# Mixture-of-experts block: both experts' sums in memory become one, and each scatter waits for the one in front of it

## The chip, the cores and the metric

The kernel runs on 1 core of one Trainium2 chip. The metric is the device time of one execution in microseconds (us), the median of several runs. A core has TensorE (PE in the rows, PEld its weight loads), VectorE (DVE), ScalarE (ACT), GpSimd (POOL) and SyncE (SP), and 16 DMA engines that serve the queues of SP, ACT and POOL. A "q" behind an engine's name (SPq, POOLq) is its sequencer.

## What is computed

Two transformer blocks over 512 tokens of width 1024. The first has a convolution and sparse attention and then a mixture of experts; the second has two mixers and two dense feed-forward nets. The change is in the experts:

```python
scores = jax.nn.sigmoid((t @ w_router).astype(jnp.float32))
_, eidx = lax.top_k(scores + router_bias.astype(jnp.float32), TOP_K_EXPERTS)
...
def expert_block(args):
    e, toks, gs = args
    xb = t[toks]
    return swiglu(xb, w1[e], w3[e], w2[e]) * gs[:, None]
...
routed = jax.ops.segment_sum(out.reshape(rows, D), row_tok, num_segments=n_tok)
shared = swiglu(t, ws1, ws3, ws2)
return (routed + shared).reshape(B, S, D)
```

Each token's row is the sum of what its 8 experts give for it, so the results of different experts are added into the same rows. 512 tokens times 8 experts over 64 experts are 64 rows for an expert on average, and up to 128 are taken at once.

## The kernel before

**One expert.** The 64 experts run one after the other in a loop that is written out (`step(n, i)`, i = 0 throughout; functions of one expert have n as argument). For expert n: GpSimd gathers its tokens' rows from memory (`gather`, L2113, tile XG, four buffers), TensorE turns them (`pe_xt`, L2007), ScalarE and VectorE split them into a high and a low part (XTh, XTl), TensorE multiplies by the up and gate weights (`pe_up`), VectorE makes silu times gate times up (`dve_hid`, L2072, tile HG, which needs the token's gate from `gate_column`, L2100, tile GS, made by GpSimd), TensorE turns that (`pe_ht`, L2032) and multiplies by the down weights (`pe_down`), ScalarE copies the 128 x 1024 result out of PSUM (`act_y`, L2091, tile YS, two buffers) and GpSimd adds it into memory (`scatter`, L2127, an indirect DMA with an addition; rows whose index is out of bounds are left out). All multiplications are three passes of 128 x 512 matmuls (L298 to L300) over weights in two parts (wh, wl), split by ScalarE (L192) and VectorE (L197) out of a ring of 12 chunks (eraw). SyncE loads the ring in pairs of chunks, 1 MB each (L1975), each when the chunks that stood there have been split: three pairs for an expert.

**Why two sums.** Even experts are added into `ysum[0]`, odd ones into `ysum[1]` (both `expert_sum` in the rows). Scatter n waits until that of n - 2, into the same sum, has landed (`y_out[s]`), then for its rows (`y_ready`). So two scatters can be in flight, into different memory. `act_y` of expert n waits for the landing of scatter n - 2 too, since it writes the same buffer of YS.

**The order on GpSimd** is fixed: in step n first `gate_column(n + 1)`, then `gather(n + 4)`, then `scatter(n)`. What stands behind scatter n on that engine, the gate of expert n + 2 and the gather of expert n + 5, is only issued after it.

**The last experts and what is over.** From n = 60 on, `more_gather` takes the place of `gather`: it copies an index column, drains (L2147) and gathers (L2153) rows for tokens beyond an expert's 128 + 64 places. These "more" blocks run after the 64 experts; with this data there are three (L2433 scatters them, each waited for, `more_gate` L2423 makes their gates). Then GpSimd waits for all scatters and tells `rows_whole`.

**Behind the experts.** Before the experts SyncE writes zeros into both sums (L1580, 8 DMAs of 512 KB). After `rows_whole` it reads both sums back (L2396, 8 DMAs of 512 KB in 4 quarters of the columns, tile YF), VectorE adds the two (L2541, 4 times 128 x 1024), TensorE turns each quarter (L2561, 8 transposes each), VectorE adds it into the residual X (`back`, L2527, twice for each quarter), ScalarE and VectorE split X (L2584, `x2_low` L2532, twice for each quarter), and the first multiplication of the second block starts. TensorE runs dummy matmuls (`keep_clock(3)`, L471) between `rows_whole` and the first transposes.

## Time and profile before

| | us |
|---|---|
| median of 3 runs | 2372.37 (2371.32 to 2376.65) |
| the profiled execution | 2377.54 |
| its span, first to last instruction | 2375.7 |
| TensorE busy in the span | 2256.5 (95%) |
| VectorE busy | 1536.6 (65%) |
| ScalarE busy | 1198.8 (50%) |
| GpSimd busy | 286.1 (12%) |
| mean granted TensorE clock | 0.983 of full |

The profiled execution took 2377.54 us, 5.17 us more than the median of the runs; its span leaves 1.84 us around it. The experts' loop takes from about 465 us (first scatter) to 1064 us (64th), the three blocks behind it until 1105 us, the second transformer block the rest. In the experts' loop the DMA engines' mean busy share is 9 tenths or more in every slice of the page; elsewhere it is mostly 1 to 3 tenths. In the rows further down, times are from the start of the span. A row of the timeline gives start, duration, engine, line, operation and tiles, and in brackets how long the engine was idle before it and what ended that. "DMA to landing" is the time from the start of the issuing instruction until all of its data has landed. The engine time of an indirect DMA on POOL is the making of its descriptors.

### The profile page before, as it was taken

How to read it: one execution, taken by the hardware profiler on the slowest of the kernel's cores; microseconds unless marked ns; L12 is line 12 of the kernel's file. 1: busy time of each engine (PE TensorE's matmuls, PEld its weight loads, DVE VectorE, ACT ScalarE, POOL GpSimd, SP SyncE). 2: the span in 40 equal slices, each digit the busy share in tenths (PEclk: the TensorE clock that was granted, in tenths of full speed). 3: DMA queues.
4: the chain of work that ended last, by engine and by line, in shares of the span. 5: the costliest groups of instructions: out<-in, count | busy, mean ns of one | idle time of the engine just before them, and what ended most of it. 6: DMA issues, size and time to landing. Idle time of an engine off the chain costs nothing.

```text
span 2375.7 us, 30540 instructions
## 1 busy us (share of the span) xinstructions
PE 2256.5 (95%) x10226; PEld 1760.5 (74%) x10226; DVE 1536.6 (65%) x2363; ACT 1198.8 (50%) x1774; POOL 286.1 (12%) x248
## 2 busy tenths in 40 slices
PE   7999999899999999985999999999999789999997
PEld 5776666778888888874766788888788557888885
DVE  7788766899999999985564643333452766433344
ACT  4432444588888888874334332333222763323333
POOL 0000000344334433431000000000020000000000
PEclk9998999999999999998999999999999999999999
DMA  8511245799999999995210132223222001322332
GB/s 330 176 59 58 80 169 172 266 354 397 388 393 387 391 392 393 391 334 156 80 63 18 62 107 96 97 97 107 89 98 98 19 27 61 116 98 92 102 106 80
DMA packets 107615, 415.70 MB, mean 175 GB/s; under 512 B 20305, under 2 KB 32849, under 8 KB 82784
## 3 DMA queue, kind: packets, MB, share of 16 engines
q1 hardware_dynamic: 87408, 378.47, 42.5%
q0 software_dynamic: 19648, 34.73, 5.9%
q8 instruction: 71, 1.16, 0.2%
q10 hardware_dynamic: 432, 0.87, 0.1%
q14 instruction: 56, 0.46, 0.1%
HBM read 409.23 MB, written 43.65 MB: 191 GB/s over the span
## 4 chain that ended last, share of the span: by engine, by line
PE 77%; DVE 9%; issue 5%; ACT 4%; DMA 2%; DVEq 2%; POOLq 0%; SPq 0%; POOL 0%; ACTq 0%
PE PS L298 22%; PE PS L300 21%; PE PS L299 21%; PE PS L714 3%; DVE wl L197 2%; PE PS L2007 2%; ACT wh L192 2%; PE PS L736 2%; PE PS L725 1%; DMA ada_wa<-wada 1%; DMA expert_sum<-YS,YIXC 1%; PE PS L2032 1%; DVE XTl L2060 1%; PE PS L1245 1%; DVEq L1285 1%
## 5 line engine op out<-in xcount | busy, mean ns | idle before, releaser
L197 DVE TENSOR_TENSOR wl<-raw,wh 128x1024 fp32r<-128x1024 f32 x239 | 292.5, 1225 | 357.2 <-ACT wh L192 351.0
L298 PE MATMUL PS<-HTh,wh 128*128 128x512 f32 x1248 | 499.9, 401 | 6.0 <-ACT V L881 2.2
L299 PE MATMUL PS<-HTl,wh 128*128 128x512 f32 x1248 | 487.8, 391 | 0.0
L300 PE MATMUL PS<-HTh,wl 128*128 128x512 f32 x1248 | 487.6, 391 | 0.0
L197 DVE TENSOR_TENSOR wl<-eraw,wh 128x1024 fp32r<-128x1024 f32 x384 | 457.7, 1219 | 16.6 <-ACT wh L192 13.6
L192 ACT ACTIVATE wh<-raw 128x1024 fp32r<-128x1024 f32 x239 | 252.0, 1056 | 369.9 <-PE PS L300 346.1
L192 ACT ACTIVATE wh<-eraw 128x1024 fp32r<-128x1024 f32 x384 | 392.6, 1054 | 17.0 <-PE PS L300 14.7
L298 PEld LDWEIGHTS PS<-HTh,wh 128*128 128x128 f32 x1248 | 235.3, 189 | 72.2 <-issue 13.6
L299 PEld LDWEIGHTS PS<-HTl,wh 128*128 128x128 f32 x1248 | 235.5, 189 | 50.2 <-issue 3.4
L300 PEld LDWEIGHTS PS<-HTh,wl 128*128 128x128 f32 x1248 | 235.3, 189 | 49.8
L298 PE MATMUL PS<-wh,XTh 128*128 128x512 f32 x536 | 221.1, 412 | 4.0 <-DVE wl L2192 2.8
L300 PE MATMUL PS<-wh,XTl 128*128 128x512 f32 x536 | 210.4, 392 | 0.0
L299 PE MATMUL PS<-wl,XTh 128*128 128x512 f32 x536 | 209.3, 390 | 0.0
L2127 POOL DMA_INDIRECT expert_sum<-YS,IDX x64 | 115.0, 1796 | 343.2 <-ACT YS L2091 211.3
L298 PE MATMUL PS<-AFh,wh 128*128 128x512 f32 x352 | 138.5, 394 | 0.0
L300 PE MATMUL PS<-AFh,wl 128*128 128x512 f32 x352 | 137.0, 389 | 0.0
L299 PE MATMUL PS<-AFl,wh 128*128 128x512 f32 x352 | 137.0, 389 | 0.0
L947 ACT ACTIVATE AFh<-AFf 128x512 f32 (+1 forms) x44 | 27.8, 632 | 182.4 <-DVEq L957 182.4
L298 PEld LDWEIGHTS PS<-wh,XTh 128*128 128x128 f32 x536 | 100.8, 188 | 23.4 <-DVE wl L2192 4.0
L300 PEld LDWEIGHTS PS<-wh,XTl 128*128 128x128 f32 x536 | 100.6, 188 | 22.2
L299 PEld LDWEIGHTS PS<-wl,XTh 128*128 128x128 f32 x536 | 101.2, 189 | 16.9
L298 PE MATMUL PS<-wh,HHh 128*128 128x512 f32 x268 | 105.6, 394 | 4.5 <-DVE HHl L2509 2.8
(412 smaller groups left out, 3439.7 us busy)
## 6 DMA issues: line engine op xcount, KB each, us to landing
eraw<-wstream SPq DMA_DIRECT2D x192, 1024.0 KB, 9.9
raw<-wstream SPq DMA_DIRECT2D x240, 512.0 KB, 3.3
ada_w<-wada SPq DMA_DIRECT2D x20, 512.0 KB, 5.9
eraw<-wexp SPq DMA_DIRECT2D x9, 1024.0 KB, 6.6
ada_wb<-wada SPq DMA_DIRECT2D x2, 2048.0 KB, 15.5
ada_l<-wada SPq DMA_DIRECT2D x8, 512.0 KB, 3.4
ada_g<-wada SPq DMA_DIRECT2D x2, 2048.0 KB, 10.3
expert_sum<-LM SPq DMA_DIRECT2D x8, 512.0 KB, 6.4
```

The costliest lines, as they stand in the source:

```text
L192: nc.scalar.activation(wh[:, ci % RING, :], src, ACT.Copy).then_inc(split_high, 1)
L197: nc.vector.tensor_tensor(wl[:, ci % RING, :], src, wh[:, ci % RING, :].bitcast(F32), ALU.subtract).then_inc(split_done, 1)
L298: nc.tensor.matmul(o, lh, rh, start=start, stop=False)
L299: nc.tensor.matmul(o, lh, rl, start=False, stop=False)
L300: return nc.tensor.matmul(o, ll, rh, start=False, stop=stop)
L714: mm = nc.tensor.matmul(PS[:, sbank(u, m), 0:P * (j + 1)], q[:, j * P:(j + 1) * P], k[:, 0:P * (j + 1)], start=x == 0, stop=x == len(prods ...
L725: mm = nc.tensor.transpose(PS[:, 4 + u % 2, kb * P:(kb + 1) * P], E_[:, u % 3, 0, kb * P:(kb + 1) * P], const("ident"))
L736: mm = nc.tensor.matmul(o, values(h, kb), Pt[:, u % 2, kb * P:(kb + 1) * P], start=kb == 0, stop=kb == j)
L947: nc.scalar.activation(ah(n, i), a_[:, n % 2, :], ACT.Copy).then_inc(s_h, 1)
L1245: nc.tensor.matmul(PS[:, 5 + n % 3, 0:P * (j + 1)], QI[b:b + HD, t, j * P:(j + 1) * P], KI[b:b + HD, 0:P * (j + 1)], start=True, stop=True ...
L2007: mm = nc.tensor.transpose(PS[:, 2 + m // 4, (m % 4) * P:(m % 4) * P + P], XG[:, n % 4, m * P:(m + 1) * P], const("ident"))
L2127: pool.indirect_dma_start(out=ysum[s], out_offset=bass.IndirectOffsetOnAxis(ap=IDX[:, 4 * n:4 * n + 1], axis=0), in_=YS[:, s, :], in_offse ...
```

## The change

One sum `ysum` takes the place of two. Scatter n now waits first for its rows (`y_ready`) and then until scatter n - 1 has landed (`y_out[1 - s]`), which is the other buffer's counter. Four DMAs write zeros, four read the sum back, the four additions on VectorE are gone, and TensorE's transposes wait for a quarter's landing. YF is half as large and stands 4096 places higher. The waits of `act_y` on its own buffer are as before.

```diff
--- before.py
+++ after.py
@@ -1563,7 +1563,7 @@
             LS = nc.alloc_sbuf_tensor_at("LS", [P, E], F32, offset=RSTD_AT + 4 * 448)
             h2rows = nc.dram_tensor("h2rows", (S, XW), F32).ap()
             blocks = nc.dram_tensor("more_blocks", (P, 3), I32).ap()
-            ysum = [nc.dram_tensor(f"expert_sum{s}", (S, D), F32).ap() for s in range(2)]
+            ysum = nc.dram_tensor("expert_sum", (S, D), F32).ap()
             EMPTY = 4103.0
 
             @stage("sp")
@@ -1576,9 +1576,8 @@
                     sp.dma_start(*expert_pair(j, EXPERT0 + j)).then_inc(expert_arrived[j // 2], 16)
                 sp.wait_ge(sem("lm_zero"), 1)
                 for tb in range(NB):
-                    for s in range(2):
-                        sp.dma_start(ysum[s].rearrange("(b p) (c e) -> b p c e", p=P, e=P)[tb],
-                                     LM[:].unsqueeze(1).broadcast_to([P, DT, P])).then_inc(sem("sum_zero"), 16)
+                    sp.dma_start(ysum.rearrange("(b p) (c e) -> b p c e", p=P, e=P)[tb],
+                                 LM[:].unsqueeze(1).broadcast_to([P, DT, P])).then_inc(sem("sum_zero"), 16)
                 sp.wait_ge(sem("gates_whole"), 1)
                 for h in range(2):
                     sp.dma_start(h2rows.rearrange("(h t p) d -> p h t d", h=2, p=P)[:, h, :, D:XW],
@@ -1706,7 +1705,7 @@
 
             def list_main(dve):
 
-                dve.wait_ge(sem("sum_zero"), 32 * NB)
+                dve.wait_ge(sem("sum_zero"), 16 * NB)
                 for b in range(2):
                     nc.vector.tensor_copy(spread_of(LM, lower)[:, b, :, :, :], ranked_of(LL, lower)[:, b, :, :, :])
                 back = LL[upper, ::-1].rearrange("p (a l H e) -> p H a l e", a=2, l=4, H=2)
@@ -1959,7 +1958,7 @@
             HHh = place("HHh", [P, 2, 256], 9472, F32R)
             HHl = place("HHl", [P, 2, 256], 9984, F32R)
             YS = nc.alloc_sbuf_tensor_at("YS", [P, 2, D], F32, offset=HT_AT)
-            YF = place("YF", [P, 2, 4, NB, 256], 3072)
+            YF = place("YF", [P, 4, NB, 256], 7168)
 
             @stage("sp")
             def _(sp):
@@ -2116,15 +2115,15 @@
 
             def scatter(pool, n, i):
                 s = n % 2
-                if n >= 2:
-                    pool.wait_ge(y_out[s], 16 * (n // 2))
-                    pool.sem_inc(passed_pool, 1)
-                elif n == 0:
-                    pool.wait_ge(sem("sum_zero"), 32 * NB)
-                    pool.sem_inc(passed_pool, 1)
                 pool.wait_ge(y_ready, i * 4 + n + 1)
                 pool.sem_inc(passed_pool, 1)
-                pool.indirect_dma_start(out=ysum[s], out_offset=bass.IndirectOffsetOnAxis(ap=IDX[:, 4 * n:4 * n + 1], axis=0),
+                if n:
+                    pool.wait_ge(y_out[1 - s], 16 * ((n + 1) // 2))
+                    pool.sem_inc(passed_pool, 1)
+                else:
+                    pool.wait_ge(sem("sum_zero"), 16 * NB)
+                    pool.sem_inc(passed_pool, 1)
+                pool.indirect_dma_start(out=ysum, out_offset=bass.IndirectOffsetOnAxis(ap=IDX[:, 4 * n:4 * n + 1], axis=0),
                                         in_=YS[:, s, :], in_offset=None, bounds_check=S - 1, oob_is_err=False,
                                         compute_op=ALU.add).then_inc(y_out[s], 16)
 
@@ -2392,9 +2391,8 @@
                 sp.wait_ge(sem("rows_whole"), 1)
                 sp.wait_ge(sem("ya_free"), 1)
                 for q in range(4):
-                    for s in range(2):
-                        sp.dma_start(YF[:, s, q, :, :], ysum[s].rearrange("(b p) (q d) -> q p b d", p=P, q=4)[q]
-                                     ).then_inc(ya_in[q], 16)
+                    sp.dma_start(YF[:, q, :, :], ysum.rearrange("(b p) (q d) -> q p b d", p=P, q=4)[q]
+                                 ).then_inc(ya_in[q], 16)
 
                 with sp.Fori(EXPERT0 // RING + 1, CHUNKS // RING - 6 * E // RING) as i:
                     for c in range(RING):
@@ -2430,7 +2428,7 @@
                     more_gather(pool, p + 2, code_of(p + 2, i), i)
                     pool.wait_ge(ov["y"], i * GROUP + (p + 2))
                     pool.sem_inc(passed_pool, 1)
-                    pool.indirect_dma_start(out=ysum[0], out_offset=bass.IndirectOffsetOnAxis(ap=YIXC[:, y:y + 1], axis=0),
+                    pool.indirect_dma_start(out=ysum, out_offset=bass.IndirectOffsetOnAxis(ap=YIXC[:, y:y + 1], axis=0),
                                             in_=YS[:, p % 2, :], in_offset=None, bounds_check=S - 1, oob_is_err=False,
                                             compute_op=ALU.add).then_inc(ov["out"], 16)
                     pool.wait_ge(ov["rows"], i * (16 * GROUP) + 16 * (p + 3))
@@ -2537,8 +2535,6 @@
                     nc.vector.tensor_scalar(lamc[:, 5:6], col("g_sub"), 1.0 - LAMBDA_INIT, None, ALU.mult)
                     dve.drain().then_inc(sem("lam_p"), 1)
                 for q in range(4):
-                    dve.wait_ge(ya_in[q], 32)
-                    nc.vector.tensor_tensor(YF[:, 0, q, :, :], YF[:, 0, q, :, :], YF[:, 1, q, :, :], ALU.add).then_inc(sem("ya_whole"), 1)
                     if second and q:
                         x2_low(2 * q - 2)
                         x2_low(2 * q - 1)
@@ -2554,12 +2550,12 @@
                 keep_clock(3)
                 for m in range(DT):
                     if m % 2 == 0:
-                        pe.wait_ge(sem("ya_whole"), m // 2 + 1)
+                        pe.wait_ge(ya_in[m // 2], 16)
                     if m >= 4:
                         pe.wait_ge(sem("ya_read"), m - 3)
                     for tb in range(NB):
                         mm = nc.tensor.transpose(PS[:, SUM_BANK[m % 4], tb * P:(tb + 1) * P],
-                                                 YF[:, 0, m // 2, tb, m % 2 * P:(m % 2 + 1) * P], const("ident"))
+                                                 YF[:, m // 2, tb, m % 2 * P:(m % 2 + 1) * P], const("ident"))
                     mm.then_inc(sem("ya_t"), 1)
 
         if second:
```

GpSimd, the scatters of experts 0 to 3 and what lies between them (XG is the gathered rows, GS the gate column, y_out0 and y_out1 count the landings of even and odd experts' scatters). Before:

```order
L2127 DMA expert_sum0<-YS_117,IDX_92 512x1024 [waits sum_zero,y_ready]
L2100 COPY GS_95<-XG_110 128x1 [waits xg_in2]
L2113 DMA XG_110<-h2rows,IDX_92 128x1088 [waits xg_in1,xt_ps,gate_at]
L2127 DMA expert_sum1<-YS_117,IDX_92 512x1024 [waits y_ready]
L2100 COPY GS_95<-XG_110 128x1 [waits xg_in3]
L2113 DMA XG_110<-h2rows,IDX_92 128x1088 [waits xg_in2,xt_ps,gate_at]
L2127 DMA expert_sum0<-YS_117,IDX_92 512x1024 [waits y_out0,y_ready]
```

Now:

```order
L2126 DMA expert_sum<-YS_117,IDX_92 512x1024 [waits y_ready,sum_zero]
L2099 COPY GS_95<-XG_110 128x1 [waits xg_in2]
L2112 DMA XG_110<-h2rows,IDX_92 128x1088 [waits xg_in1,xt_ps,gate_at]
L2126 DMA expert_sum<-YS_117,IDX_92 512x1024 [waits y_ready,y_out0]
L2099 COPY GS_95<-XG_110 128x1 [waits xg_in3]
L2112 DMA XG_110<-h2rows,IDX_92 128x1088 [waits xg_in2,xt_ps,gate_at]
L2126 DMA expert_sum<-YS_117,IDX_92 512x1024 [waits y_ready,y_out1]
```

No instruction has moved; the odd expert's scatter, which waited for no landing or for that of two experts ago, now waits for the even one's just in front of it, and the other way round.

VectorE, behind the experts (YF is the sum read back, X the residual, HTl its low part). Before:

```order
L2537 TENSOR_SCALAR lamc<-C 128x1
L2541 TENSOR_TENSOR YF<-YF 128x1024 [waits ya_in0]
L2527 SCALAR_TENSOR_TENSOR X<-PS,cond,X 128x512 [waits ya_t] x2
L2541 TENSOR_TENSOR YF<-YF 128x1024 [waits ya_in1]
L2532 TENSOR_TENSOR HTl<-X,HTh 128x512 [waits x2h] x2
L2527 SCALAR_TENSOR_TENSOR X<-PS,cond,X 128x512 [waits ya_t] x2
```

Now:

```order
L2535 TENSOR_SCALAR lamc<-C 128x1
L2525 SCALAR_TENSOR_TENSOR X<-PS,cond,X 128x512 [waits ya_t] x2
L2530 TENSOR_TENSOR HTl<-X,HTh 128x512 [waits x2h] x2
L2525 SCALAR_TENSOR_TENSOR X<-PS,cond,X 128x512 [waits ya_t] x2
```

The additions have gone from between the others, here the first two of four.

## Rows read from the trace of the kernel before

**Rows 1.** Start of scatter 1 to 59: length, PE, PEld, DVE, ACT, POOL, clock, DMA, GB/s.
```profile
475.22:1024.97 549.75, 546.23 (x2674) 448.78 (x2673) 529.21 (x595) 488.38 (x581) 219.61 (x176) 1.00 1.02 387
```

**Rows 2.** Timeline of POOL, a scatter in the loop and the gate behind it.
```profile
760.75 2.08 POOL L2127 DMA_INDIRECT expert_sum<-YS,IDX  x1 [6.29 <-ACT YS L2091]
762.27 1.71 POOL L2100 COPY GS<-XG 128x1 f32<-128x1 f32 x1
```

**Rows 3.** DMA issues from 470 to 530 us: count, size, median us to landing.
```profile
eraw<-wstream SPq DMA_DIRECT2D x18, 1024.0 KB, 7.7
expert_sum<-YS,IDX POOLq DMA_INDIRECT x6, 9.4
```

**Rows 4.** DMA issues from 530 to 710 us.
```profile
eraw<-wstream SPq DMA_DIRECT2D x58, 1024.0 KB, 9.5
expert_sum<-YS,IDX POOLq DMA_INDIRECT x19, 9.2
```

**Rows 5.** DMA issues from 710 to 890 us.
```profile
expert_sum<-YS,IDX POOLq DMA_INDIRECT x19, 9.6
```

**Rows 6.** The scatters of the three blocks behind the experts (L2433), shortest, median, longest.
```profile
DMA to landing us min/median/max: 5.1/6.0/6.3
```

**Rows 7.** Timelines of ACT and POOL: the rows are ready, the scatter starts.
```profile
503.51 1.03 ACT L2091 ACTIVATE YS<-PS 128x1024 f32<-128x1024 f32 x1 [1.11 <-PE PS L300]
505.42 2.18 POOL L2127 DMA_INDIRECT expert_sum<-YS,IDX  x1 [6.62 <-DVE HG L2072]
```

**Rows 8.** Timeline of DVE: the hidden row that needs the gate just made.
```profile
768.62 0.47 DVE L2072 SCALAR_TENSOR_TENSOR HG<-SG,GS,PS 128x256 f32<-128x256 f32 x1
```

**Rows 9.** Timeline, the last experts: scatters 61 and 63, ACT's copy 63, gate, hidden row.
```profile
1052.68 1.60 POOL L2127 DMA_INDIRECT expert_sum<-YS,IDX  x1 [0.31 <-issue]
...
1062.41 1.03 ACT L2091 ACTIVATE YS<-PS 128x1024 f32<-128x1024 f32 x1 [4.61 <-DMA expert_sum<-YS,IDX]
...
1064.27 1.56 POOL L2127 DMA_INDIRECT expert_sum<-YS,IDX  x1 [8.04 <-ACT YS L2091]
1065.24 1.55 POOL L2423 COPY GS<-XG 128x1 f32 x1
...
1069.16 0.48 DVE L2506 SCALAR_TENSOR_TENSOR HG<-SG,GS,PS 128x256 f32<-128x256 f32 x1
```

**Rows 10.** Scatter 63 (L2127) alone, issued at 1064.27: shortest, median, longest.
```profile
DMA to landing us min/median/max: 5.5/5.5/5.5
```

**Rows 11.** Timeline of SP, its first issue after the zeros.
```profile
413.67 0.91 SPq L1584 DMA_DIRECT2D h2rows<-G  x2
```

**Rows 12.** Timeline behind the experts: reading back, adding, turning, first matmul of block 2.
```profile
1108.08 8.78 SPq L2396 DMA_DIRECT2D YF<-expert_sum  x8
1108.11 4.66 PE L471 MATMUL PS<-K 128*128 128x512 f32 x6 [10.05 <-POOLq L2445]
1115.30 1.23 DVE L2541 TENSOR_TENSOR YF<-YF 128x1024 f32<-128x1024 f32 x1 [9.61 <-DMA YF<-expert_sum]
1116.58 1.97 PE L2561 MATMUL PS<-K,YF 128*128 128x128 f32 x8 [3.81 <-DVE YF L2541]
1117.74 1.60 DVE L2527 SCALAR_TENSOR_TENSOR X<-PS,cond,X 128x512 f32<-128x512 f32 x2 [1.21 <-PE PS L2561]
1130.46 0.77 PE L298 MATMUL PS<-HTh,wh 128*128 128x512 f32 x1
1131.09 1.47 DVE L2532 TENSOR_TENSOR HTl<-X,HTh 128x512 fp32r<-128x512 f32 x2
```

**Rows 13.** Landing of the eight reads of YF: shortest, median, longest.
```profile
DMA to landing us min/median/max: 3.4/8.1/10.1
```

**Rows 14.** Timeline of PE in the tail: an idle time and a matmul soon after it.
```profile
1055.05 0.44 PE L2032 MATMUL PS<-K,HG 128*128 128x128 f32 x2 [2.74 <-DVE HG L2072]
1057.65 0.63 PE L299 MATMUL PS<-wl,HHh 128*128 128x512 f32 x1
```

**Rows 15.** Page, costliest groups: the matmuls of L299 in the loop; busy us, mean ns.
```profile
L299 PE MATMUL PS<-wl,XTh 128*128 128x512 f32 x536 | 209.3, 390 | 0.0
```

## The prediction, made before the changed kernel was run

> **What bounds the kernel now.** I read first the busy time of each engine in the stretch that the change touches, the experts' loop. From the start of scatter 1 to that of scatter 59 are 549.75 us; TensorE is busy for 546.23 of them at a granted clock of 1.00 [rows 1]. That is 549.75 / 58 = 9.48 us for an expert, and TensorE sets it. The DMA engines are full at the same time (share 1.02, 387 GB/s) [rows 1], with the stream of weights above all. The reader is to see that both are full, and that GpSimd, with 219.61 us, is not.
>
> Then GpSimd's timeline, for what a step does there: scatter at 760.75, gate of the expert after next from 762.27 to 763.98 [rows 2]. The scatter waits for its rows, not for a landing. Then the DMA issues by stretch, for how long a scatter is under way: median 9.4 us, 9.2, 9.6 [rows 3 to 5]. This is the number that matters: a landing takes almost exactly as long as an expert. With two sums nobody waits for it, since the wait is for the landing of two experts ago, 9.5 us more. With one sum it becomes a link of a chain.
>
> **The wait that is added.** Scatter n may only start when n - 1 has landed, so two scatters stand at least a landing and a wake-up apart. The wake-up is not shown for a landing; its nearest row is the wake-up by ScalarE: the copy YS ends at 503.51 + 1.03 = 504.54, the scatter starts at 505.42 [rows 7], 0.88 us. The instructions between are the same two waits and the setting of a register, so I take 0.88.
>
> The landing under the new pace is shown by no row. Bounds: 6.0 us, the median of the three scatters behind the loop, which have little beside them [rows 6], and 9.6, the worst stretch [rows 5]. I take 9.2 [rows 4]. It is nearest to the stretches in the loop, since the same 3 MB of weights an expert stay beside it. At a step of some 10 us the stream asks for 6% less, which speaks for the low one of the three medians; but between 470 and 530 us the stream's own transfers landed in 7.7 us, against 9.5 later, and the scatters were no faster there, 9.4 against 9.2 [rows 3, 4]. So I don't go below 9.2.
>
> A step then takes 9.2 + 0.88 = 10.08 us in place of 9.48, 58 of them 584.6 us: **+34.9 us** in GpSimd's time at scatter 59.
>
> **What is queued behind the wait.** On GpSimd the gate of expert n + 2 and the gather of n + 5 stand behind scatter n. The gather has three experts of time. The gate has less: it ended at 763.98, and VectorE's hidden row that needs it started at 768.62 [rows 2, 8], 4.6 us of slack. GpSimd falls behind by 0.6 us an expert, so the slack is used up after some 8 experts; from then on TensorE waits for VectorE's hidden row about 0.6 us in each. Does the slack of 4.6 us come off the sum? No: in the tail GpSimd is already what the others wait for (TensorE idle for 2.74 us until HG, whose gate stands behind scatter 61 [rows 14]), so its lag is passed on whole.
>
> **The tail.** Scatters 60 and 61 stand behind drains of `more_gather` and are apart by more than a landing already. Scatter 62 followed 61 closely and must now wait for it. ScalarE's copy 63 waits for the same landing and starts at 1062.41 [rows 9]; scatter 62 then starts at about 1063.2. Alone it lands in 5.5 us [rows 10], at 1068.7, and scatter 63 starts at 1069.6 in place of 1064.27 [rows 9]: 5.3 us later. The gate behind it ended 2.5 us after the scatter's start, which makes 1072.1, and the hidden row that needs it ran at 1069.16 [rows 9]: 2.9 us at least. The first extra block's gather and scatter stand behind too. I take **+5 us**, between 3 and 7. The three extra blocks wait for each landing already; nothing there.
>
> **What is removed.** Zeroing: 4 DMAs less for SyncE. That gives nothing: what SyncE issues next waits for the router's gates and starts at 413.67 [rows 11], whether it has issued 4 or 8 before. If the gates came sooner than the eighth, the four would be worth their issue time, some us.
> Reading back: the first addition starts at 1115.30, 7.2 us after the first of 8 reads was issued [rows 12], as two of them must land and share the engines with the rest. A single one lands in 3.4 us [rows 13], at 1111.5. TensorE's dummies end at 1112.77 [rows 12], so its transposes start there, not at 1116.58: -3.8 us. Further on VectorE sets the pace: from 1117.74 to 1132.56 [rows 12] it runs 8 `back`, 8 low parts and 3 additions of 1.23. Without these it is done 3.7 + 3.8 = 7.5 us earlier. TensorE, whose last transposes no longer queue behind an addition, can start the next matmuls (1130.46 before) up to 11 us earlier, but needs the last low parts soon. I take **-9 us**, between -7 and -11.
>
> **Sum.** +34.9 + 5 - 9 = +31 us. On the profiled execution (2377.5) this gives 2408; that one was 5.2 us over the median of the runs, so on the median 2372.4 + 31 = **2403 us**.
>
> **Rivals.**
> A, the landing gives way. If scatters land faster once each runs alone in its sum, the chain may be shorter than TensorE's step. It decides at 9.48 - 0.88 = 8.6 us a landing: below that nothing is lost in the loop, and the tail and the end leave 5 - 9 = -4 us to -7 us: about 2366, faster. For it: alone, 6.0 us [rows 6], so a third of a landing is made by company, and a slower loop makes the stream thinner: some feedback is certain. Against it: in the loop a scatter never had much company of another scatter, and no stretch has a median below 9.2. The Trainium skill, "DMA: Bandwidth & Descriptors", Anatomy of one DMA (SWDGE path), gives about 2.0 us plus bytes / 436e3 for such a DMA; by that rule, as an estimate, 262 KB for 64 rows would land in 2.6 us, the wait would be free and the sum would be A's 2366. The trace doesn't agree even for scatters nearly alone (5.1 to 6.3 us) [rows 6]. 0.13.
>
> B, the landing doesn't change at all and is 9.6 us [rows 5] throughout: 58 x 10.48 = 607.8, +58, with the rest +54: 2426. This is the upper end of my own forecast.
>
> C, the clock. Today an idle time of 2.74 us was followed by matmuls at 0.63 us each [rows 14], where the mean of such matmuls is 0.39 [rows 15]. If 0.6 us idle an expert were enough for that, some nine matmuls an expert would cost 0.2 us more each, 1.8 us, of which 0.6 lie in the wait: +70 us more, about 2473. Against it: the granted clock is 1.00 with the small gaps of today [rows 1]. 0.04.
>
> D, the lag isn't passed on: the tail's drains of many us could swallow the 4.6 us that GpSimd is behind. Then 2398, inside the range.
>
> **Numbers.** The forecast (landing 8.75 to 9.6 us) has 0.80; A 0.13; C and what else is slower 0.07. The range: at 8.75 us, 58 x 9.63 = 558.5, +8.8 + 5 - 9 = +5, 2377; at 9.6 us 2426. The time of no change is reached at a landing of 8.67 us. A measurement of this kernel can tell about 0.2%, 4.7 us, from no change. Faster by over that (most of A) 0.10; within 0.08 (the rest of A, landings near 8.7); slower 0.82.
>
> **What would show it.** In the profile after: scatters 10.1 us apart; landings of 9 us or more; POOL idle before L2126 until DMA expert_sum, no longer until ACT YS; VectorE's HG waiting for POOL GS some 50 times for about 0.6 us, and TensorE for HG; DMA share in the loop about 0.95; clock 1.00. Behind the experts YF's reads landing within some 8 us of the first issue, and the first matmul of block 2 about 17 us after the first read was issued, against 22.4 today. The prediction is wrong if the landings fall under 8.7 us, if HG doesn't wait in the loop, or if the span from scatter 1 to 59 grows by less than 9 or more than 60 us.

## The result, and the profile after

The changed kernel takes 2422.51 us (median of 4 runs, 2417.3 to 2426.81), the kernel before in the same rounds 2374.51 us (4 runs, 2371.32 to 2380.21). The ratio is 1.0195, 95% interval [1.018, 1.0209]: 46 us slower (43 to 50; the two medians are 48 apart), where +31 was forecast. It is slower, and the time lies in the range, at its upper end. The profiled execution is the fastest of the four, 2417.3 us for a span of 2415.5, and that span is 39.8 us over the one before.

The page of the changed kernel: span, busy time, and of its part 4 the shares of the chain that ended last, by engine and by line.

```profile
span 2415.5 us, 30529 instructions
...
PE 2267.9 (94%) x10226; PEld 1764.9 (73%) x10226; DVE 1534.2 (64%) x2359; ACT 1200.7 (50%) x1774; POOL 285.8 (12%) x248
...
PE 59%; DMA 25%; DVE 6%; issue 5%; ACT 2%; DVEq 1%; POOLq 1%; POOL 0%; SPq 0%; ACTq 0%
DMA expert_sum<-YS,IDX 23%; PE PS L298 17%; PE PS L300 16%; PE PS L299 16%; PE PS L714 3%; PE PS L736 2%; PE PS L725 1%; DMA ada_wa<-wada 1%; DMA expert_sum<-YS,YIXC 1%; DVEq L1285 1%; DVE wl L197 1%; DVE M L1282 1%; PE PS L1245 1%; ACT wh L192 0%; DVE X L648 0%
```

The same two lines of the page before:

```profile
PE 77%; DVE 9%; issue 5%; ACT 4%; DMA 2%; DVEq 2%; POOLq 0%; SPq 0%; POOL 0%; ACTq 0%
PE PS L298 22%; PE PS L300 21%; PE PS L299 21%; PE PS L714 3%; DVE wl L197 2%; PE PS L2007 2%; ACT wh L192 2%; PE PS L736 2%; PE PS L725 1%; DMA ada_wa<-wada 1%; DMA expert_sum<-YS,YIXC 1%; PE PS L2032 1%; DVE XTl L2060 1%; PE PS L1245 1%; DVEq L1285 1%
```

This is the shortest way to see what happened. 23% of the span, 556 us, are now a chain of scatters' landings, an entry that was not among the lines before. It has taken the place of the experts' matmuls. TensorE still shows as busy for 94%, so its busy share alone would hide this.

The loop, from scatter 1 to scatter 59, answers to [rows 1]: length, PE, PEld, DVE, ACT, POOL, granted clock, DMA share, GB/s.

```profile
471.79:1066.21 594.42, 562.51 (x2694) 458.17 (x2693) 534.91 (x599) 493.19 (x584) 217.85 (x177) 0.98 0.99 361
```

594.4 us in place of 549.8, so 10.25 us for an expert in place of 9.48. The scatter's line in this stretch, first what ended GpSimd's idle time ahead of it (us, times), then the time from issue to landing:

```profile
  DMA expert_sum<-YS,IDX: 354.2, 55
  issue: 12.6, 3
  ACT YS L2090: 6.0, 1
...
DMA to landing us min/median/max: 5.8/9.1/12.8
```

Of 59 scatters 55 were released by a landing. The last line has the landings of the even experts' scatters only; over all of the loop they are 5.1 to 12.8 us, with a median of 9.2. The waits of the same stretch (engine, line, waited for: us in total, times, longest) tell how that reaches TensorE:

```profile
POOL expert_sum L2126 <- DMA expert_sum<-YS,IDX: 354.2, 55, 10.3
...
PEld PS L2031 <- DVE HG L2071: 45.6, 35, 3.6
DVE HG L2071 <- POOL GS L2099: 34.4, 24, 3.0
PE PS L2031 <- DVE HG L2071: 30.4, 21, 3.2
```

Scatter, the gate behind it on GpSimd, the hidden row on VectorE, the matmuls of TensorE. In one step it looks like this. GpSimd's timeline, and below it VectorE's:

```profile
741.32 1.83 POOL L2126 DMA_INDIRECT expert_sum<-YS,IDX  x1 [8.27 <-DMA expert_sum<-YS,IDX]
742.60 0.75 POOL L2099 COPY GS<-XG 128x1 f32<-128x1 f32 x1
...
749.68 1.89 POOL L2126 DMA_INDIRECT expert_sum<-YS,IDX  x1 [5.09 <-DMA expert_sum<-YS,IDX]
```

```profile
743.39 0.48 DVE L2071 SCALAR_TENSOR_TENSOR HG<-SG,GS,PS 128x256 f32<-128x256 f32 x1 [1.72 <-POOL GS L2099]
```

The gate ends at 743.35 and the hidden row starts at 743.39, after 1.72 us of idle time. Before, 4.6 us lay between them [rows 2, 8].

The wake-up by a landing, which no row of before showed, stands in the chain of waits near scatter 59 (start, us, what):

```profile
1055.16 10.19 DMA expert_sum<-YS,IDX
...
1066.50 0.22 POOL expert_sum L2126
```

Scatter 58 landed at 1065.35, and scatter 59 started at 1066.21 (below): 0.86 us, against 0.88 taken from the wake-up by ScalarE [rows 7].

The tail answers to [rows 9]; scatters 59 to 64 in GpSimd's timeline:

```profile
1066.21 1.60 POOL L2126 DMA_INDIRECT expert_sum<-YS,IDX  x1 [5.70 <-DMA expert_sum<-YS,IDX]
...
1083.30 1.60 POOL L2126 DMA_INDIRECT expert_sum<-YS,IDX  x1 [0.31 <-issue]
...
1093.43 2.56 POOL L2126 DMA_INDIRECT expert_sum<-YS,IDX  x1 [0.31 <-issue]
...
1100.36 1.58 POOL L2126 DMA_INDIRECT expert_sum<-YS,IDX  x1 [3.56 <-DMA expert_sum<-YS,IDX]
1110.96 1.56 POOL L2126 DMA_INDIRECT expert_sum<-YS,IDX  x1 [9.02 <-DMA expert_sum<-YS,IDX]
...
1123.84 2.49 POOL L2431 DMA_INDIRECT expert_sum<-YS,YIXC  x1 [0.30 <-issue]
```

Scatter 62 stands 6.9 us behind 61, where it stood 2.0 us before, and 63 stands 10.6 us behind 62, where it stood 9.6. The end answers to [rows 12]:

```profile
1156.24 2.32 SPq L2394 DMA_DIRECT2D YF<-expert_sum  x4
1156.27 5.49 PE L471 MATMUL PS<-K 128*128 128x512 f32 x6 [13.07 <-POOLq L2443]
...
1161.55 3.11 PE L2557 MATMUL PS<-K,YF 128*128 128x128 f32 x24
1162.52 1.41 DVE L2525 SCALAR_TENSOR_TENSOR X<-PS,cond,X 128x512 f32<-128x512 f32 x2 [11.71 <-PE PS L2557]
...
1167.33 0.48 PE L298 MATMUL PS<-HTh,wh 128*128 128x512 f32 x1
```

From the first read to the first matmul of block 2 are 11.1 us, where it was 22.4. Four reads landed within 3.5 to 6.8 us each, against 3.4 to 10.1 for eight [rows 13].

The span, cut where the two executions can be told apart (starts of scatters, of the first read, and of the first result of block 2's first product):

| stretch | before | after | difference | forecast |
|---|---|---|---|---|
| start to scatter 1 | 475.2 | 471.8 | -3.4 | 0 |
| scatter 1 to 59 | 549.8 | 594.4 | +44.7 | +34.9 |
| scatter 59 to 64 | 51.0 | 57.6 | +6.6 | +5 |
| scatter 64 to first read | 32.1 | 32.4 | +0.3 | 0 |
| first read to block 2's first result | 33.8 | 21.6 | -12.2 | -9 |
| the rest | 1233.9 | 1237.7 | +3.8 | 0 |
| span | 2375.7 | 2415.5 | +39.8 | +31 |

The first and the last row differ by as much between runs: in the twelve experiments below they are 469.4 to 477.5 and 1232.4 to 1241.5 us. Nothing in them is the change's.

### The profile page after: what moved, and what is told of

Same layout as the page of the kernel before. It is cut to its first block, busy times and chain, and to the rows that moved or that the text cites. A ratio compares the mean times of both kernels' runs of the same rounds, so it can differ in the third digit from the quotient of the medians.

```text
span 2415.5 us, 30529 instructions
## 1 busy us (share of the span) xinstructions
PE 2267.9 (94%) x10226; PEld 1764.9 (73%) x10226; DVE 1534.2 (64%) x2359; ACT 1200.7 (50%) x1774; POOL 285.8 (12%) x248
## 4 chain that ended last, share of the span: by engine, by line
PE 59%; DMA 25%; DVE 6%; issue 5%; ACT 2%; DVEq 1%; POOLq 1%; POOL 0%; SPq 0%; ACTq 0%
DMA expert_sum<-YS,IDX 23%; PE PS L298 17%; PE PS L300 16%; PE PS L299 16%; PE PS L714 3%; PE PS L736 2%; PE PS L725 1%; DMA ada_wa<-wada 1%; DMA expert_sum<-YS,YIXC 1%; DVEq L1285 1%; DVE wl L197 1%; DVE M L1282 1%; PE PS L1245 1%; ACT wh L192 0%; DVE X L648 0%
## 5 line engine op out<-in xcount | busy, mean ns | idle before, releaser
L299 PE MATMUL PS<-HTl,wh 128*128 128x512 f32 x1248 | 486.8, 390 | 0.0
L299 PEld LDWEIGHTS PS<-HTl,wh 128*128 128x128 f32 x1248 | 234.7, 188 | 49.9 <-issue 3.4
L299 PE MATMUL PS<-wl,XTh 128*128 128x512 f32 x536 | 212.1, 396 | 0.0
L2126 POOL DMA_INDIRECT expert_sum<-YS,IDX x64 | 126.3, 1974 | 393.7 <-DMA expert_sum<-YS,IDX 366.8
L299 PE MATMUL PS<-AFl,wh 128*128 128x512 f32 x352 | 137.0, 389 | 0.0
L299 PEld LDWEIGHTS PS<-wl,XTh 128*128 128x128 f32 x536 | 102.7, 192 | 17.3
## 6 DMA issues: line engine op xcount, KB each, us to landing
ada_g<-wada SPq DMA_DIRECT2D x2, 2048.0 KB, 10.1
```

What stands on the lines that cost most here:

```text
L299: nc.tensor.matmul(o, lh, rl, start=False, stop=False)
L2126: pool.indirect_dma_start(out=ysum, out_offset=bass.IndirectOffsetOnAxis(ap=IDX[:, 4 * n:4 * n + 1], axis=0), in_=YS[:, s, :], in_offset=N ...
```

## Experiments

For every run these numbers are told: the loop (scatter 1 to 59; 549.8 before, 594.4 after), the tail (59 to 64; 51.0 and 57.6), the end (scatter 66 to block 2's first result; 41.9 and 30.3), and the mean landing in the loop (9.45 us before). In a chain that mean is the step less the rest of the link; after the change it is 10.25 - 0.88 = 9.37, and the landings read one by one have a mean of 9.36.

**1. The wait alone.** The kernel before, with its two sums and its eight reads, and only scatter's waits as in the change:

```diff
-                if n >= 2:
-                    pool.wait_ge(y_out[s], 16 * (n // 2))
...
                 pool.wait_ge(y_ready, i * 4 + n + 1)
                 pool.sem_inc(passed_pool, 1)
+                if n:
+                    pool.wait_ge(y_out[1 - s], 16 * ((n + 1) // 2))
```

> Two sums as before, but scatter n waits for the landing of n - 1, as in the changed kernel. Theory 1 (the wait alone makes the loop longer: a landing of about 9.4 us plus 0.88 us of wake-up is the step): scatters 1 to 59 take 590 to 600 us as in the changed kernel, the tail is as in the changed kernel, the reading back as before, so the time is about 2374 + 45 + 7 = 2426. Theory 2 (adding into one region of memory makes a scatter slower): the landings stay apart in two regions, so the step falls back towards 9.5 to 9.9 us and the time is under 2400.

Measured: 2426.19 us, ratio 1.0188 [1.0163, 1.0212]; loop 596.0, tail 53.6, end 40.4. Its scatters in the loop:

```profile
  DMA expert_sum<-YS,IDX: 348.2, 55
...
DMA to landing us min/median/max: 6.2/9.2/13.1
```

The same 55 waits for a landing and the same loop as the change, with two sums in memory. So the loop's cost is the wait's, and that scatters meet in the same memory costs nothing in the loop that shows. The tail is a warning: by the same waits it is 53.6 here and 57.6 in the change.

**2. One read alone.** The kernel before, two sums, of which one is read back; what the odd experts give is left out:

```diff
-                    for s in range(2):
-                        sp.dma_start(YF[:, s, q, :, :], ysum[s].rearrange("(b p) (q d) -> q p b d", p=P, q=4)[q]
-                                     ).then_inc(ya_in[q], 16)
+                    sp.dma_start(YF[:, 0, q, :, :], ysum[0].rearrange("(b p) (q d) -> q p b d", p=P, q=4)[q]
+                                 ).then_inc(ya_in[q], 16)
...
-                    dve.wait_ge(ya_in[q], 32)
-                    nc.vector.tensor_tensor(YF[:, 0, q, :, :], YF[:, 0, q, :, :], YF[:, 1, q, :, :], ALU.add).then_inc(sem("ya_whole"), 1)
...
```

> The kernel before with the end of the changed one: only the sum of the even experts is read back (4 DMAs), no additions on VectorE. It leaves out what the odd experts give. Theory 1: the end alone is worth 12 us, as the traces of before and after show between the first read and the first result of the second block: about 2362. The prediction's term was 9 us: 2365. If the reading back were hidden: 2374.

Measured: 2364.25 us, ratio 0.9937 [0.992, 0.9954], 15 us less (11 to 19); loop 549.6, tail 50.6, end 29.6. The end alone is 12.3 us shorter, as in the change. Experiments 1 and 2 together are the change, but for the one memory that is added into. Their ratios multiply to 1.012, about 30 us, and the change's is 1.0195, 46 us; even the outer ends of the intervals don't meet (1.0165 against 1.018). In the traces most of this gap is gone: loop +46.2 and -0.1, tail +2.6 and -0.4, end -1.5 and -12.3 make +34.5, against +39.7 of the change in the same three, and 4.4 us of the rest are the tail's. What makes the tail differ is open; "Sum" below comes back to the ratios.

**3 and 4. A delay in the chain, and the same one where there is no chain.** A fill of unused space on GpSimd, which is waited for ahead of each scatter, in the changed kernel and in the one before:

```diff
+                nc.gpsimd.memset(SCR[:], 0.0).then_inc(sem("dly"), 1)
+                pool.wait_ge(sem("dly"), n + 1)
+                pool.sem_inc(passed_pool, 1)
                 pool.indirect_dma_start(out=ysum, out_offset=bass.IndirectOffsetOnAxis(ap=IDX[:, 4 * n:4 * n + 1], axis=0),
```

> The changed kernel with a 128 x 512 memset on GpSimd, waited for, between the landing of scatter n - 1 and scatter n (some 0.5 to 1 us, its length to be read from the trace, plus a wake-up). Theory 1: the chain of landings sets the loop, so each of the 58 steps grows by the whole of it: +30 to +60 us over the changed kernel. Theory 3 (the loop is held by TensorE, slowed by a lower clock and by waits, and GpSimd only follows): less than a third of that.

> The kernel before with the same memset between the rows being ready and the scatter. No landing is waited for there and GpSimd is idle for 5 us in each step, so both theories say no change in the loop: 2374, at most 3 us more from the tail. More than 10 us would mean that engine time of GpSimd by itself (its share of memory ports with VectorE) costs, and that the run with the delay in the chain must be read less that.

In the change: 2436.38 us, ratio 1.0239 [1.0218, 1.026]; loop 613.5, tail 59.2. In the kernel before: 2382.19 us, ratio 1.0014 [1.0002, 1.0025]; loop 549.8, tail 54.5. GpSimd's timeline in the change with the delay:

```profile
703.39 0.53 POOL L2127 MEMSET SCR<- 128x512 f32 x1 [4.32 <-DMA expert_sum<-YS,IDX]
704.80 1.61 POOL L2130 DMA_INDIRECT expert_sum<-YS,IDX  x1 [0.88 <-POOL SCR L2127]
```

Off the chain the delay is hidden in the whole loop; 3.5 us show in the tail. On the chain the fill starts 0.15 us after a landing on the mean, where a scatter starts 0.88 after it; with the fill's 0.53 and 0.90 from its end to the scatter a link has 1.58 us besides the landing: 0.70 more, which over 58 links would be 41 us. The loop grew by 19.1 us, the run by 14. That is less than the 30 to 60 us that were expected for a chain, and by that scale it would speak for the other theory, that TensorE holds the loop. The trace decides against it: 56 of the 58 fills in the loop were released by a landing, and no scatter of it started more than 2.5 us after the landing in front of it, so the landings and what lies between them are the whole loop. What the expectation had wrong is that a landing stays as long as it was. The mean landing had fallen to 10.58 - 1.58 = 8.99 us. So the chain sets the time, but it isn't stiff; experiment 12 takes this further.

**5 and 6. A thinner stream.** Half of each pair of weights is loaded, so TensorE computes with other numbers, in the changed kernel and in the one before:

```diff
-                        sp.dma_start(*expert_pair(j, i * ER + (EXPERT0 + j))).then_inc(expert_arrived[j // 2], 16)
+                        o, a = expert_pair(j, i * ER + (EXPERT0 + j))
+                        sp.dma_start(o[:, 0:CW], a[:, 0:CW]).then_inc(expert_arrived[j // 2], 16)
```

> The changed kernel with half of each pair of weight chunks loaded from the second round of the ring on (512 KB in place of 1 MB, the same number of DMAs); the other half of a chunk pair keeps older weights, so its result is another. Theory 1 (the landing is long because the stream of weights shares the DMA engines, and the chain of landings is the loop): landings fall to about 7 us, under the 8.6 us from which TensorE sets the step again; the loop from scatter 1 to 59 is 550 us as before the change, and the time about 2374 + 7 - 12 = 2369. If the landing is long for another reason (the making of descriptors, the addition itself): landings above 9, loop 590 us, time 2420.

> The kernel before with the same thinner stream, as the comparison for it. TensorE set the step before, so all theories say loop 550 us and 2370 to 2376; landings about 7 us by theory 1. If it were much faster than 2370, the stream of weights would have been a bound before the change too.

With the change: 2365.45 us, ratio 0.9949 [0.9932, 0.9967]; loop 550.0, tail 50.8, end 28.8. Without: 2374.75 us, ratio 0.9997 [0.9985, 1.0009]; loop 549.7, tail 49.0, end 43.0. The loop of the first, and what ended GpSimd's idle time ahead of its scatters:

```profile
469.40:1019.30 549.90, 546.19 (x2673) 448.72 (x2673) 529.74 (x595) 488.69 (x580) 217.74 (x176) 1.00 0.79 222
```

```profile
POOL expert_sum L2127 <- ACT YS L2091: 148.9, 28, 5.9
POOL expert_sum L2127 <- DVE HG L2072: 106.7, 19, 6.7
POOL expert_sum L2127 <- DMA expert_sum<-YS,IDX: 60.9, 10, 6.7
```

The stream has fallen from 361 to 222 GB/s and the mean landing to 7.37 us. 7.37 + 0.88 = 8.25 lies under TensorE's 9.48, and the loop costs nothing: scatters wait for their rows again. Loading less is worth nothing in the kernel before, so what this gives the change, some 57 us, is the landing's alone. This is rival A with its condition made true, and its time (2366 forecast, 2365 measured) came too.

**7. A scatter of half as many places.** The changed kernel; what an expert gives for tokens beyond its first 64 places is left out:

(HALF is 64.)

```diff
-                pool.indirect_dma_start(out=ysum, out_offset=bass.IndirectOffsetOnAxis(ap=IDX[:, 4 * n:4 * n + 1], axis=0),
-                                        in_=YS[:, s, :], in_offset=None, bounds_check=S - 1, oob_is_err=False,
+                pool.indirect_dma_start(out=ysum, out_offset=bass.IndirectOffsetOnAxis(ap=IDX[0:HALF, 4 * n:4 * n + 1], axis=0),
+                                        in_=YS[0:HALF, s, :], in_offset=None, bounds_check=S - 1, oob_is_err=False,
```

> The changed kernel, but a scatter takes only the first 64 of the 128 rows (it leaves out the results of tokens beyond an expert's first 64 places). Theory 1: the last part of a landing is the rows' transfer in turn with the stream, so half the rows land some 2 us sooner, about 7.2 us, under 8.6; the loop is 550 us and the time about 2365 to 2370. If the landing is mostly fixed cost (issue to first packet and receipt): 8.5 to 9 us, the loop 555 to 575 us, the time 2375 to 2400.

Measured: 2366.24 us, ratio 0.995 [0.9932, 0.9969]; loop 550.0, tail 51.3, end 29.2. The mean landing is 7.39 us:

```profile
DMA to landing us min/median/max: 4.2/7.4/9.2
```

The stream is at 374 GB/s here, so 64 places fewer take as much off a landing (2.0 us) as 40% of the stream's rate does. Not all of these places held a row. The page's line of GpSimd's queue (packets, MB, share) in the change, and below it in this run:

```profile
q0 software_dynamic: 19648, 34.73, 6.0%
q0 software_dynamic: 15552, 26.77, 4.3%
```

4,096 packets are gone, one for each of 64 places in 64 scatters, but only 7.96 MB: 124 KB a scatter, 30 rows of 4 KB, so 34 of the 64 places were empty. The Trainium skill, "DMA: Bandwidth & Descriptors", Anatomy of one DMA, gives bytes / 436e3 for what grows with the size: as an estimate, 0.3 us for 124 KB. The trace doesn't agree with that for this DMA, as it didn't with the fit's level. How the 2.0 us divide between the 30 rows and the 34 empty places is told by no run.

**8. Gates one expert earlier.** The changed kernel, with the gate of expert n + 2 ahead of scatter n in place of behind it:

```diff
                 more_counts(pool)
+                gate_column(pool, 1)
...
-                    if n + 1 < E:
-                        gate_column(pool, n + 1)
+                    if n + 2 < E:
+                        gate_column(pool, n + 2)
```

> The changed kernel, but GpSimd makes the gate of expert n + 2 ahead of scatter n, so that no gate stands behind a wait for a landing. Theory 1 (the chain of landings is the loop): the stall only moves, from VectorE's hidden row to ScalarE's copy of the result, which needs a landing too; scatters 1 to 59 take 590 to 597 us, time 2415 to 2423. Theory 4 (the price is the gates queued behind the late scatter): the loop falls to 550 to 565 us, time 2375 to 2390.

Measured: 2407.77 us, ratio 1.0117 [1.0089, 1.0146]; loop 589.9, tail 52.1, end 31.4. What GpSimd waited for in the loop:

```profile
POOL expert_sum L2126 <- DMA expert_sum<-YS,IDX: 267.9, 46, 8.6
POOL expert_sum L2126 <- DVE HG L2071: 73.7, 11, 8.6
```

The chain holds without the gate: ScalarE's copy YS waited 21 times, 29.7 us, for a landing, TensorE 15 times, 20.5 us, for the gather XG, and the loop keeps a step of 589.9 / 58 = 10.17 us. The tail is 5.5 us shorter than in the change, but 4.8 us of that lie between scatters 59 and 61, where GpSimd's drains were shorter, and not behind a late gate; and experiment 1 has 4.0 us less with the gates where they were. So this run doesn't tell what the gates are worth in the tail. Its time lies between what the two theories had (2415 to 2423, and 2375 to 2390), its loop just below the first one's 590; it is 1.2% slower than the kernel before.

**9, 10 and 11. Keeping two sums and shortening the end.** Three attempts to have the gain at the end without the chain. The kernel before, whose odd sum is read while the extra blocks run (9); the same, and the even sum is added onto it by accumulating reads, with no additions on VectorE (10); the first with gates one expert earlier (11). The early read of 9, and below it the accumulating reads of 10:

```diff
+                sp.wait_ge(y_out[1], 16 * E // 2)
+                for q in range(4):
+                    sp.dma_start(YO[:, q, :, :], ysum[1].rearrange("(b p) (q d) -> q p b d", p=P, q=4)[q]
+                                 ).then_inc(ya_in[q], 16)
                 sp.wait_ge(sem("rows_whole"), 1)
...
+                for q in range(4):
+                    pool.dma_start(YO[:, q, :, :], ysum[0].rearrange("(b p) (q d) -> q p b d", p=P, q=4)[q],
+                                   accum_op=ALU.add).then_inc(ya_in[q], 16)
```

> Two sums and the waits of before. The odd experts' sum, complete after scatter 63, is read back (4 DMAs of 512 KB) while the extra blocks run; behind them only the even sum is read, and VectorE adds as before. Theory 1: the first quarter is there 3.4 us after its issue in place of 7.2 us for two, so the end is 3.8 us shorter, against about 1 us that the early reads may cost the extra blocks: 3 us less than before, ratio 0.999. If the four reads lengthen the extra blocks' scatters more than that: no gain.

> As the early read, but the even sum is added onto the odd one by GpSimd's DMAs (4 accumulating DMAs into on-chip memory), and VectorE's four additions are gone. Theory 1: the end is as in the changed kernel (12 us shorter) if an accumulating DMA of 512 KB lands as soon as a plain one; 4096 rows of 1 KB for software descriptors may take 3 to 6 us more for each quarter, which would leave between 0 and 9 us of it. I expect 2368 to 2376 for a before of 2376.

> The early read with the gates made one expert earlier on GpSimd too. Two sums, so the loop doesn't wait for landings and stays at 550 us; the gates of experts 62 and 63 no longer stand behind the drains and late scatters of the tail, where TensorE waited 1.1 and 2.7 us for hidden rows: another 2 to 4 us, about 6 us less than before, ratio 0.9975. If the tail is held by the drains alone: as the early read.

| run | us | ratio | loop | tail | scatter 64 to 66 | end |
|---|---|---|---|---|---|---|
| before | 2378.49 | | 549.8 | 51.0 | 24.0 | 41.9 |
| 9 | 2376.14 | 0.9991 [0.9982, 1.0001] | 549.7 | 52.2 | 26.1 | 38.5 |
| 10 | 2379.74 | 1.0005 [0.9996, 1.0014] | 549.8 | 51.6 | 26.0 | 38.3 |
| 11 | 2380.10 | 1.0003 [0.9993, 1.0013] | 549.7 | 51.3 | 26.8 | 38.1 |

None is told from no change, so the gains expected of 10 (up to 9 us) and 11 (about 6) did not come. The end is 3.4 to 3.8 us shorter, and 2.0 to 2.8 of it are lost again between scatters 64 and 66, where the early reads run. In 9 the four additions still set VectorE's pace. In 10 the transposes (PE, out of the read buffer) wait for each accumulating read:

```profile
1108.58 5.34 POOL L2447 DMA_DIRECT2D YO<-expert_sum  x4 [8.60 <-issue]
...
1114.48 1.09 PE L2562 MATMUL PS<-K,YO 128*128 128x128 f32 x8 [0.99 <-DMA YO<-expert_sum]
...
1117.35 1.78 PE L2562 MATMUL PS<-K,YO 128*128 128x128 f32 x8 [1.78 <-DMA YO<-expert_sum]
...
1120.01 1.97 PE L2562 MATMUL PS<-K,YO 128*128 128x128 f32 x8 [0.87 <-DMA YO<-expert_sum]
```

They come 2.7 to 2.9 us apart; the additions they replace take 1.23 us each.

**12. Three delays in the chain.** As 3, with three fills, each waited for. Asked was whether the landing keeps giving way.

```diff
+                for h in range(3):
+                    nc.gpsimd.memset(SCR[:], 0.0).then_inc(sem("dly"), 1)
+                    pool.wait_ge(sem("dly"), 3 * n + h + 1)
```

> The changed kernel with three waited-for memsets in the chain, about 2.1 us by the one memset's 0.70 us. With one, the loop grew by 19 us and not by 41, since the landings got shorter (about 9.0 us after 9.4). If landings go on giving way as the step grows, they fall to 7.5 to 8.5 us and the loop takes 620 to 665 us; if they have a floor near 9: 58 x (9.0 + 0.88 + 2.1) = 695 us.

Measured: 2479.15 us, ratio 1.0423 [1.0404, 1.0442]; loop 653.8, tail 59.6, end 29.2. The loop's window:

```profile
474.20:1128.00 653.80, 580.69 (x2702) 470.84 (x2700) 537.03 (x600) 499.19 (x588) 300.08 (x350) 0.96 0.94 330
```

| run | step | link besides the landing | mean landing |
|---|---|---|---|
| before (no chain) | 9.48 | | 9.45 |
| the change | 10.25 | 0.88 | 9.37 |
| one fill | 10.58 | 1.58 | 8.99 |
| three fills | 11.27 | 2.95 | 8.32 |

Between the last three, 2.07 us more in a link give a step 1.02 us longer and a landing 1.05 us shorter: half of a longer link is given back.

**Not tried:** one sum with the old waits, which would be the gain at the end for nothing. Two scatters under way could then add into the same row at once; that no addition is lost by it is shown by no run. Of the eight experiments that compute the whole result none beats the kernel before; the others (2, 5, 6, 7) leave out part of it.

## Why the prediction came out as it did

**The mechanism held at each link.** Scatter, landing, wake-up, next scatter: experiment 1 puts the whole loop's cost on the wait, and experiments 3, 5 and 7 move it by the landing or the link alone. Rival A's condition (a landing under 8.6 us) is tested by experiments 5 and 7: at 7.4 us the loop costs nothing, at 9.4, in the change, it costs 45.

**The term that was mis-sized is the landing**, taken at 9.2 us. 9.2 was the lowest median of three stretches [rows 4]. From scatter 1 to 63 the landings of the kernel before were:

```profile
DMA to landing us min/median/max: 5.5/9.3/11.5
```

A chain of 58 landings takes 58 times their mean, and the mean over the loop was 9.45, with a median of 9.3: long ones of up to 11.5 us count in it more than in the median. The mean after was 9.37, with a median of 9.2. The difference of 0.17 is 58 x 0.17 = 10 us, the whole of what the loop missed (44.7 against 34.9). It is made of three parts: 0.1 for the choice of the stretch, 0.15 for the median in place of the mean, and less 0.08 by which the landings gave way. With 9.45 the same sum would have given 58 x 10.33 - 549.75 = +49, and with 9.3 it would have given +41.

**The wake-up of 0.88 us held** (0.86 in the row above), though it was taken from a wake-up by another engine.

**The lag did not stay where it was put.** GpSimd was to be 4.6 us behind and then hold, which with the 0.9 us of before would put a scatter 5.5 us behind its ready rows. It was 6.6 us behind them on average and 12.0 at most. The hidden row waited 24 times and 34.4 us in all, up to 3.0 at once, where about 50 waits of 0.6 us were forecast. Landings of 5.1 to 12.8 us make a lag that grows and shrinks; the sum over the loop is the same, since the chain sets it.

**The clock.** The granted clock of the loop was 0.98, where 1.00 was forecast, and the DMA share 0.99 (361 GB/s) in place of 0.95. The matmuls on XTh and XTl went from means of 412, 390 and 393 ns to 417, 395 and 398, those on HHh and HHl stayed at 390. That is rival C in small: some 1,400 matmuls by 5 ns are 7 us of TensorE's busy time. They cost nothing here, since TensorE was waiting for the chain; 0.98 of 2.4 GHz means that few matmuls ran at the lower level.

**The tail, forecast at +5, measured +6.6.** Of that 5.5 us stand between scatters 59 and 63, where 5.3 were worked out, the rest in the drain behind 63. But two errors cancel in it. The working let scatter 62 start 8.5 us later, behind the 9.6 us that 61 took to land before; 61 now landed after 6.1 us (1093.43 to 1099.50), and 62 started 4.5 us later against scatter 59. And it let 62 land alone in 5.5 us, where it took 9.8 (1100.36 to 1110.14). Experiment 1, with the same waits, has 2.6 us for the whole tail. A forecast of 3 to 7 was right about the size; the agreement to the tenth is luck.

**The end, forecast at -9, measured -12.2 and in experiment 2 -12.3.** Two bounds were worked out: VectorE done 7.5 us earlier, TensorE's next matmuls starting up to 11 us earlier, and a value between them was taken. Both bounds held: VectorE ended its last low part 24.5 us after the first read before [rows 12] and 17.2 us after it now (1172.10 + 1.35), 7.3 us less, and the matmuls started after 11.1 us in place of 22.4, 11.3 us less. The step that failed is "but needs the last low parts soon", and with it the 17 us named as the start of block 2. The transposes were done at 1167.3 (24 of the 32 in one row of 3.11 us), the matmuls followed at once, and no wait for a low part shows until the first result, which came 10.5 us later. Before, it was 11.4 us, and the first of these matmuls took 0.77 us [rows 12] where it takes 0.48 now. TensorE's windows (stretch, length, busy, granted clock, DMA share, GB/s) show why, of before the transposes, the first matmuls of block 2 and the next ones:

```profile
1116.60:1130.40 13.80, 7.87 (x34) 0.50 0.73 253
1130.46:1134.00 3.54, 3.54 (x13) 0.74 0.00 0
1134.00:1141.80 7.80, 7.80 (x36) 1.00 0.21 67
```

and of after the same:

```profile
1161.50:1167.30 5.80, 4.34 (x35) 0.94 1.06 398
1167.33:1171.00 3.67, 3.67 (x19) 1.00 0.11 40
```

Waiting for the additions, TensorE ran its transposes at 0.50, the lower of its two levels (1.2 GHz), and kept it into the first 3.5 us of block 2. 3.54 us at 0.74 instead of 1.00 are 0.9 us, the rest of the gain. The single transposes say the same, with a median of 421 ns before, 273 ns after and 273 ns in experiment 2.

**The zeroing** gave nothing, as forecast: SyncE's next issue came at 411.04 with the four DMAs at 391.68, a wait for the gates in between [rows 11].

**Sum.** +44.7 + 6.6 - 12.2 = +39.1 from the change's own stretches, against +31; the 8 us between them are 9.8 of the loop and 1.6 of the tail, less 3.2 of the end. The runs show +46. The experiments put the profiled pair's +39.8 nearer to the truth. In all twelve the change of time by the ratio and by the traces' stretches agree within 3.5 us; taking what the traces have between each one on the changed kernel, or experiment 1, and the change off its ratio gives the change itself, as an estimate, as +36 to +41. The first rounds, where +46 was measured, are the only ones out of line. They had the lowest median of the kernel before, 2374.51 us with 4 runs, against 2376.25 to 2379.88 us beside the experiments, and single runs of the changed kernel spread over 9 us. Why they differ stays open.

## What to carry to other kernels

When a wait turns work that overlapped into a chain, its price is the mean of a link times their number, so take the mean of the duration over the whole stretch and not the median of a part of it, and add the wake-up. Compare that sum with what the other engines need for a step: under it the wait is free, over it each tenth of a microsecond is multiplied by the loop's length, and a saving that is made once, behind the loop, has to be as large as that product: here it was 12 us against 45. And before slack is added elsewhere, ask whether the chain has any: here gates one expert earlier took 4.5 of the loop's 44.7 us away.

## What the runs showed of the hardware that was not expected

- **A landing gives way, but late.** From a step of 9.48 to one of 10.25 us the mean landing fell by 0.08 us; from 10.25 to 11.27 by 1.05 (experiments 3 and 12), with the stream's rate at 387, 361, 348 and 330 GB/s. That a scatter finds the DMA engines fuller while the stream still catches up is an explanation that fits, not one that was tested.
- **Places cost as much as company.** A scatter of 64 places in place of 128 (30 rows and 34 empty places fewer) and 40% less of the stream both took 2.0 us off a landing.
- **What 0.88 us between a landing and a scatter is.** A fill on GpSimd started 0.15 us after the landing that it waited for, the scatter 0.88 after a landing, a fill or ScalarE's copy alike (experiments 3 and 12, [rows 7]). So most of the 0.88 is not the wake-up by a landing but comes with the scatter itself.
- **A drain of GpSimd ends with the scatter under way.** The chain of waits of the kernel before, and the landing of the scatter that it issued at 1040.87:

```profile
1040.33 3.05 POOLq L2147
1043.70 6.04 issue
```

```profile
DMA to landing us min/median/max: 8.7/8.7/8.7
```

  The scatter landed at 1049.6, and GpSimd went on at 1049.74. In the change the scatter at 1083.30 landed after 7.8 us, at 1091.1, and GpSimd went on at 1091.23. In the twelve experiments the same drain ended 0.13 us after the landing of the same scatter too (0.31 in 6). So in this kernel a drain behind a scatter is a wait for its landing, 9 us here for the copying of one column of indices, and this is why the tail held such a chain before the change. The first drain of each pair ended 4.46 us after the landing of scatter 59, before and after the change and in eleven of the twelve experiments (5.04 in 7). What fills these 4.46 us was not found.
- **Accumulating reads into on-chip memory** of 512 KB each come 2.7 to 2.9 us apart; in the changed kernel four plain ones of the same size, issued within 2.3 us, were each done in 3.5 to 6.8 us from their issue.
